# Latent attention: rotary's exchanged copy by a VectorE permutation of partitions instead of two output tiles of the query projection

## The reference, cut to what matters

```
cq  = rms_norm(h @ w_cq) (512 x 384);  ckv = rms_norm(h @ w_ckv) (512 x 256)
q   = cq @ even_w_uq      8 heads of 64 plain + 32 rotary features
k,v = ckv @ even_w_ukv    8 heads of 64 + 64; 32 rotary key features shared by all heads
rope(x): x1, x2 = halves of 16;  [x1*cos - x2*sin, x2*cos + x1*sin]
out = concat(plain heads, softmax(q k^T / sqrt(96), causal) v) @ even_w_out
```

## Time and profile before

| | before |
|---|---|
| median of 3 runs | 1935.88 us (1934.05 to 1936.56) |
| span of the profiled execution | 1933.6 us, 2.3 us under the median of the runs |
| the profiled execution's own time | not among the times shown; what lies around its span is about the 2.3 us |
| instructions | 30753 |
| TensorE matmuls busy | 1914.8 us (99%) |
| VectorE busy | 1156.5 us (60%) |
| ScalarE busy | 818.0 us (42%) |

### The profile page before, as it was taken

One profiled execution on the slowest core, in us unless ns is written; L12 is line 12 of the kernel. 1 busy time (PEld: TensorE's weight loads), 2 busy tenths in 40 slices (PEclk: granted clock), 3 DMA queues, 4 the chain that ended last, 5 costly groups with the idle time before them and its releaser, 6 DMA issues.

```text
span 1933.6 us, 30753 instructions
## 1 busy us (share of the span) xinstructions
PE 1914.8 (99%) x12210; PEld 1567.9 (81%) x12210; DVE 1156.5 (60%) x1891; ACT 818.0 (42%) x1327; POOL 27.4 (1%) x31
## 2 busy tenths in 40 slices
PE   9999999999999999999999999999999999999998
PEld 7777788888888877788888888877888778888887
DVE  6556577533655766657652555789988666425532
ACT  5457554333334454445332333465555543212232
POOL 0111000000000000000000000000000000000000
PEclk9999999999999999999999999999999999999999
DMA  6222123223223211131223222322111132322321
GB/s 222 77 77 77 49 83 107 78 98 109 89 88 128 71 45 66 66 109 66 87 87 109 104 83 82 112 67 79 56 62 46 66 109 87 109 87 88 108 87 66
DMA packets 30804, 168.61 MB, mean 87 GB/s; under 512 B 6456, under 2 KB 6616, under 8 KB 14816
## 3 DMA queue, kind: packets, MB, share of 16 engines
q1 hardware_dynamic: 25872, 161.69, 24.2%
q10 hardware_dynamic: 4816, 5.29, 0.9%
HBM read 163.78 MB, written 2.13 MB: 86 GB/s over the span
## 4 chain that ended last, share of the span: by engine, by line
PE 85%; DVE 8%; ACT 4%; issue 2%; DMA 1%; SPq 0%; DVEq 0%; ACTq 0%
PE bank L523 25%; PE bank L525 24%; PE bank L524 24%; PE bank L806 1%; ACT hH L1378 1%; PE bank L1172 1%; DVE hL L2194 1%; PE bank L989 1%; ACT wH L1378 1%; PE bank L818 1%; DVE x L2190 1%; PE bank L829 1%; PE bank L1013 1%; DVE wL L2117 1%; PE bank L1263 1%
## 5 line engine op out<-in xcount | busy, mean ns | idle before, releaser
L523 PE MATMUL bank<-hH,wH 128*128 128x512 f32 x1368 | 550.0, 402 | 1.8 <-DVE hL L2156 1.4
L525 PE MATMUL bank<-hH,wL 128*128 128x512 f32 x1368 | 532.1, 389 | 0.0
L524 PE MATMUL bank<-hL,wH 128*128 128x512 f32 x1368 | 531.4, 388 | 0.0
L1378 ACT ACTIVATE wH<-raw 128x2048 fp32r<-128x2048 f32 (+3 forms) x199 | 294.1, 1489 | 120.0 <-PE bank L525 104.8
L523 PEld LDWEIGHTS bank<-hH,wH 128*128 128x128 f32 x1368 | 257.2, 188 | 61.4 <-issue 9.1
L525 PEld LDWEIGHTS bank<-hH,wL 128*128 128x128 f32 x1368 | 256.8, 188 | 54.7
L2108 DVE TENSOR_TENSOR wL<-raw,wH 128x2048 fp32r<-128x2048 f32 x96 | 219.7, 2289 | 134.6 <-ACT wH L1378 134.6
L524 PEld LDWEIGHTS bank<-hL,wH 128*128 128x128 f32 x1368 | 257.5, 188 | 47.6 <-issue 1.2
L523 PE MATMUL bank<-mH,wH 128*128 128x512 f32 (+1 forms) x610 | 232.8, 382 | 0.0
L525 PE MATMUL bank<-mH,wL 128*128 128x512 f32 (+1 forms) x610 | 232.6, 381 | 0.0
L524 PE MATMUL bank<-mL,wH 128*128 128x512 f32 (+1 forms) x610 | 232.6, 381 | 0.0
(11 more groups left out here) (355 smaller groups left out, 2724.5 us busy)
## 6 DMA issues: line engine op xcount, KB each, us to landing
raw<-in_ffn_up SPq DMA_DIRECT2D x44, 1024.0 KB, 4.9
raw<-in_mlp_up SPq DMA_DIRECT2D x16, 1024.0 KB, 4.9
raw<-in_mlp_down SPq DMA_DIRECT2D x16, 1024.0 KB, 4.9
raw<-in_ffn_down SPq DMA_DIRECT2D x16, 768.0 KB, 4.3
raw<-in_odd_in SPq DMA_DIRECT2D x12, 1024.0 KB, 4.9
raw<-in_dn_qkv SPq DMA_DIRECT2D x12, 1024.0 KB, 5.0
raw<-in_ffn_down SPq DMA_DIRECT2D x16, 640.0 KB, 3.9
raw<-in_even_in SPq DMA_DIRECT2D x7, 1024.0 KB, 4.9
```

The source lines that it names most:

```text
L523: mm(out, a, c, start=first, stop=False, skip_group_check=joined)
L524: mm(out, a, d, start=False, stop=False, skip_group_check=joined)
L525: return mm(out, b, c, start=False, stop=last, skip_group_check=joined)
L1378: return nc.scalar.activation(out, in_, func, **kw)
```

## The change

The exchanged tiles go: the query projection has six output tiles, three for each unit, and a unit is 1152 columns wide. The exchanged copy is made by VectorE from the plain tile's bank, by `stream_shuffle` with the list 16..31, 0..15 within each quadrant of 32 partitions, and VectorE waits for it before the sine product, which then reads it from SBUF. The query projection's slots end at 178 instead of 184; everything behind is moved up: pairs 16, 17, 18 by two slots (172, 174, 176), pairs 19 and up and the output projection by three. Slots 178 to 180 have no projection step on TensorE. The second unit is needed at slot 169. Its split stays at slots 161 to 166. On VectorE rotary of group 0 moves to slot 163 (behind the division of pair 14) with its addition at once, that of group 1 to slot 175 with its addition at once, ahead of division 16 (176), the low part of group 3 (176) and minimum 18 (176). Bank 1 is now free for the next tile with the permutation's end (`rope.turned`).

```diff
-STREAMS = [("even_in", 9, 2048), ("even_ukv", 1, 2048), ("even_uq", 2, 1536), ("even_out", 4, 2048)]
+STREAMS = [("even_in", 9, 2048), ("even_ukv", 1, 2048), ("even_uq", 2, 1152), ("even_out", 4, 2048)]
-TILES = {"even_uq": 8, "even_ukv": 4 + 4}
+TILES = {"even_uq": 6, "even_ukv": 4 + 4}
...
-            return (48, 76, 104, 147)[g] + (7, 7, 7, 6)[g] * n if g < 4 else (174, 176, 178)[n] if m < 19 else 172 + 3 * (m - 16)
+            return (48, 76, 104, 147)[g] + (7, 7, 7, 6)[g] * n if g < 4 else (172, 174, 176)[n] if m < 19 else 169 + 3 * (m - 16)
...
-            return 16 * n - 14 if n < 9 else (130, 146, 161, 174, 186)[n - 9]
+            return 16 * n - 14 if n < 9 else (130, 146, 161, 171, 183)[n - 9]
...
-            for t in range(160, 184):
+            for t in range(160, 178):
                 j, k = (t - 160) // 3, (t - 160) % 3
-                n = UNIT0["even_uq"] + j // 4
+                n = UNIT0["even_uq"] + j // 3
                 pair_events(t)
                 if k == 0:
-                    if j % 4 == 0:
+                    if j % 3 == 0:
                         pe.wait_ge(w_split, n + 1)
-                    pe.wait_ge(*at(("ukv.out5", "ukv.out6", "ukv.out7", "rope.cos0", "rope.sin0", "uq.nope0", "uq.nope1", "rope.cos1")[j]))
-                c = slice(k * 512 + (j % 4) * P, k * 512 + (j % 4) * P + P)
+                    pe.wait_ge(*at(("ukv.out5", "ukv.out6", "ukv.out7", "rope.turned0", "uq.nope0", "uq.nope1")[j]))
+                c = slice(k * 384 + (j % 3) * P, k * 384 + (j % 3) * P + P)
...
-                if t < 220:
-                    n = (t - 184) // 3
-                    return None if t % 3 != 1 else (n // 8, n // 4 % 2, n % 4)
-                t -= 220
+                if t < 217:
+                    n = (t - 181) // 3
+                    return None if t < 181 or t % 3 != 1 else (n // 8, n // 4 % 2, n % 4)
+                t -= 217
...
-            for t in range(184, 240):
+            for t in range(178, 237):
...
-                if t in (170, 173, 182, 185):
-                    p = (170, 173, 182, 185).index(t)
-                    j = (2, 3, 6, 7)[p]
+                if t in (167, 170, 176, 179):
+                    p = (167, 170, 176, 179).index(t)
+                    j = (1, 2, 4, 5)[p]
...
-                turned, plain = (bank[uq_bank(4 * g + 1 - a_)][:] for a_ in range(2))
-                done("even_uq", 4 * g)
+                plain = bank[uq_bank(3 * g)][:]
+                done("even_uq", 3 * g)
                 if g:
                     dve.wait_ge(*at("rope.rotated0"))
                 stt(sq[:, g, :], plain, s, rope[:, 0, :], ALU.mult, ALU.mult).then_inc(*tick("rope_dve", f"rope.cos{g}"))
-                done("even_uq", 4 * g + 1)
-                stt(ss[:], turned, s, rope[:, 1, :], ALU.mult, ALU.mult).then_inc(*tick("rope_dve", f"rope.sin{g}"))
+                chain(nc.vector.stream_shuffle(ss[:], plain, [*range(16, 32), *range(16)]), "rope_dve", f"rope.turned{g}")
+                stt(ss[:], ss[:], s, rope[:, 1, :], ALU.mult, ALU.mult).then_inc(*tick("rope_dve", f"rope.sin{g}"))
...
-                if t in (166, 178):
-                    rotary((t - 166) // 12)
+                if t == 175:
+                    rotary(1)
                 for m in pairs_at(t, 4):
                     pair_divided(m)
+                if t == 163:
+                    rotary(0)
+                    rotated(0)
...
-                if t in (166, 178):
-                    rotated((t - 166) // 12)
+                if t == 175:
+                    rotated(1)
```

More of the change, by code:

```diff
@@ L943, in _ @@
                         pe.wait_ge(w_split, UNIT0["even_out"] + u + 1)
-                    pe.wait_ge(*at(("rope.sin1", "uq.nope2", "uq.nope3", "pair.biased31.1")[2 * u + tl]))
+                    pe.wait_ge(*at(("uq.nope3", "rope.turned1", "uq.nope2", "pair.biased31.1")[2 * u + tl]))
                 pe.wait_ge(*at(f"pair.out{k}"))
@@ L1656, in even_hi @@
             def even_hi(n, f):
-                act.wait_ge(mm_done, 2 * n - 2 if n <= 10 else TILE0["even_uq"] + 4 * (n - 11))
+                act.wait_ge(mm_done, 2 * n - 2 if n <= 10 else TILE0["even_uq"] + 3 * (n - 11))
                 hi_half(n, f)
@@ L1690, in rank_square @@
                 a(dst, cqRaw[:, k, :], ACT.Square).then_inc(*tick("norm_act", f"cq.sq{k}"))
-            for t in range(34, 240):
+            for t in range(34, 237):
                 for n in range(3, 14):
@@ L1696, in _ @@
                             even_hi(n, f)
-                if t == 222:
+                if t == 219:
                     act.wait_ge(*at("pair.scores31.1"))
@@ L1735, in _ @@
                     pair_hi(g)
-                if t == 188:
-                    act.wait_ge(*at("rope.sin1"))
+                if t == 185:
+                    act.wait_ge(*at("rope.turned1"))
                     a(small[:, 8:9], eps, ACT.Copy).then_inc(evac, TILES["even_ukv"] + TILES["even_uq"])
@@ L2479, in _ @@
                     for f in range(2):
-                        if (203 if (n, f) == (13, 1) else even_split_half(n, f) + 3 + f) == t:
+                        if (200 if (n, f) == (13, 1) else even_split_half(n, f) + 3 + f) == t:
                             lo_half(n, f)
-                if t == 226:
+                if t == 223:
                     lo_half(14, 0)
@@ L3068 @@
         four = heads[4 * g:4 * g + 4]
-        cols += [wq[:, 64:] for wq in four] + [np.concatenate([wq[:, 80:], wq[:, 64:80]], 1) for wq in four]
-        cols += [wq[:, :64] for wq in four]
-    arrays["even_uq"] = units(np.concatenate(cols, 1), 512)
+        cols += [wq[:, 64:] for wq in four] + [wq[:, :64] for wq in four]
+    arrays["even_uq"] = units(np.concatenate(cols, 1), 384)
     arrays["even_ukv"] = units(a["even_w_ukv"][0].reshape(256, H, 2, 64).transpose(0, 2, 1, 3).reshape(256, 1024), 1024)
```

## The result

The changed kernel takes 1941.68 us (median of 8 executions, 1939.86 to 1942.84), the kernel before, run beside it, 1936.62 us (median of 8, 1934.05 to 1938.49). The ratio is 1.0026, 95% interval 1.0017 to 1.0034: slower by 5.1 us, outside of the predicted range of 1932.6 to 1937.6. The profiled execution took 1942.52 us with a span of 1940.7, 7.1 us more than the span before. Around the span of every execution whose span is on record lie 1.7 to 1.9 us. So the profiled execution of the kernel before took about 1935.4 us, and what lies around its span is not the 2.3 us that the table of before has.

A forecast was written before the change was run, and what follows sets the result against it. TensorE, busy for 99% of the span, was taken as the bound: 4.1 us of steps and 0.3 of old idle time go, 4.1 of new idle time come, a 0.4 us lead, so 1935.5 us, range 1932.6 to 1937.6.

The forecast's parts named there:

- The sum over the stage's order: Latent-heads stage: 4.1 us of steps and 0.3 of old idle go, 4.1 of new idle come, lead 0.4 us.
- Permutation: VectorE, once per group: the 128x512 permutation takes 0.71 us, range 0.42 to 1.21, taken from the 32x32 transposition.
- rival (b): VectorE's permutation is dear and the kernel slower: 12 in 100 for above 0.91 us, 2 in 100 for above 2.9.
- Rotary: VectorE: cosine 0.60, permutation 0.71 + 0.04, sine 0.71, addition 0.60, together 2.66 us.
- The end of the weight unit: VectorE: the second half of the second weight unit's split ends at 162.81, where TensorE waits for it at slot 169.
- Stalls: New TensorE idle time: 2.5 us at slot 169, 0.5 before the scores of pair 19, 1.1 before pair 20.
- Rival (a): Stage: the saving comes through whole, 4.4 us go, 1931.5 us, 0.23% faster; 7 in 100, with half-way cases.
- rival (c): The stall at slot 169 lowers TensorE's clock; under 1 us at 1.2 GHz eats the 0.4; 3 in 100.
- 8 us at 1.2 GHz would be needed for 1939.5: TensorE's clock: every microsecond at 1.2 GHz loses half a microsecond of work, so 1939.5 us needs 8 us of it.
- the first stall: TensorE at slot 169 waits for the second half of VectorE's weight split, from 160.34 until 162.9: 2.5 us idle.
- a lead of 0.4: Followed along the path through the stage, the changed kernel is 0.4 us ahead: pair 21 at 182.4, not 182.83.
- I let the 0.4 us stand to the end: From slot 181 on: all engines' lists are unchanged, three slots sooner, so the 0.4 us lead stays: 1935.5 us.

The follow-up runs named there:

- e10: The changed kernel with 12 TensorE instructions (three one-column matmuls) put back at slot 190 and nothing else; 1939.15 us, ratio 1.0013.
- e3: The kernel before with the first half of the second unit's split done two times more on VectorE, so TensorE has to wait; 1940.58 us, ratio 1.0018.
- e4: The changed kernel with 36 TensorE instructions put back at 650 us, nine one-column sums in a norm of the second block; 1941.70 us, ratio 1.0026.
- e1: The changed kernel with GpSimd's clearing of qM and kM held until VectorE's division of pair 14 is done; 1938.86 us, ratio 1.0011.
- e6: The kernel before with 18 matmuls left out, 36 TensorE instructions fewer as in the changed kernel, every order kept; 1940.26 us, ratio 1.0018.
- e9: The changed kernel with GpSimd's clearing later, rotary of group 1 and one split half sooner, 12 TensorE instructions put back at slot 190; 1935.04 us, ratio 0.9993.
- e5: The changed kernel with GpSimd's clearing behind pair 14's division and 36 TensorE instructions (nine one-column matmuls) put back at slot 180; 1938.13 us, ratio 1.0006.
- e8: The changed kernel with GpSimd's clearing later, rotary of group 1 and one split half sooner, 36 TensorE instructions put back in the stage; 1935.71 us, ratio 0.9998.
- e2: The kernel before with only the last of three steps of each exchanged tile computed, 12 matmuls left out, all orders kept; 1936.76 us, ratio 1.0004.

## Why the prediction was wrong

**What held.** The sum over the stage's order was right in its steps. Permutation: 0.71 forecast, 0.73 measured, so rival (b) falls, whose point was 0.91. Rotary: 2.66, measured 2.71. The end of the weight unit: 162.8, measured 162.6. Stalls: 2.5, 0.5 and 1.1, measured 2.41, 0.30 and 0.84, each with the releaser named. The two later ones are shorter because TensorE itself was slower: from pair 17 to being ready for pair 19 it needed 7.61 us (169.79 to 177.40) where 7.3 was forecast, and from pair 19 to being ready for pair 20 1.70 where 1.46. Rival (a) falls with the 2.41 us: the saving did not come through. Up to pair 21 the sum's result is right too: the changed kernel's loss there, 1.3 us from its own start, is the 1.7 of clock less 0.4. To the end it isn't, even at full clock: e10's two executions without a fall are 0.9 us over those of before, of which its filling explains 0.7.

On the permutation's price the Trainium skill's figure (VectorE: DVE Perf Modes, The perf-mode tier table) gave an estimate of 0.60 us. The trace has 0.73 and decides. The same page (The DRAIN you can't avoid) gives no extra cost for a semaphore between two chained instructions. Here an instruction whose result is awaited is followed after 0.72 us (158.49 to 159.21), one whose result isn't after 0.61 (159.21 to 159.82), so the trace doesn't agree.

**First step that failed: rival (c), at 3 in 100.** The wait at slot 169 lowers the clock; it should have been part of the forecast. The text took the earlier trace rows, a wait of 2.12 us with full clock behind it, as evidence that such a wait is harmless. It was one execution, and the kernel before had a mean clock of 1.000 in only 15 of 83 others. The same wait is followed by the lower clock in the profiled executions of 9 of the 11 other kernels. The text also reckoned that 8 us at 1.2 GHz would be needed for 1939.5, without asking how long a fall lasts. Here each takes 1.7 us of work (3.4 us at half speed), in the stage as in the third block, but for the two long ones of e3 and e4. That makes the first stall 4.1 us and not 2.4, and all four traces with a wait of 2.3 to 2.5 us in the stage (the changed kernel, e3, e4, e10) have the fall. The 1.7 us turn a lead of 0.4 into a loss of 1.3, which is what pair 21 shows. By itself this step would have given 1937.2 us, within the range. e1 and e3 show it from both sides: without the wait the fall goes, with a wait in the kernel before it comes.

**Second step that failed: "I let the 0.4 us stand to the end".** The text reasoned that behind the stage all lists are the same, three slots sooner. The lead was gone at 187 us, in part by a wait of 0.23 us for ScalarE's copy y, which the kernel before doesn't have. And the instructions are the same, but there are 36 fewer ahead of them, and with that TensorE stands still in the third block. It costs 2.2 us of waiting and 1.7 us of clock, 3.9 us, which is more than half of the 7.1 us between the two spans, and no part of the forecast had a term for it. By the times it is 2.5 us (1941.68 to 1939.15, the changed kernel against e10), with e10's filling, 0.7 us, and its larger loss at 1228 (0.4 more) in the way. The 0.8 us at 1228 to 1232, a loss that only kernels with fewer instructions have, belong here too. e6 shows that taking instructions out is enough to bring the wait for issue up, e10 that 12 put back take it away.

**The sum as it came out**, in the span: 1.0 us at pair 21, that is 1.3 of the stage less the 0.3 by which this trace is ahead from its start; 0.4 more to 187 us; 0.8 at 1228 to 1232 us; 1.3 for that execution's clock fall behind the wait of 1296; 3.9 for the wait for issue and its clock fall; and 0.3 come back by 1400. Together 7.1, as between the spans. The profiled execution of before had no fall, and many of its others have some, so the medians show less, 5.1.

What stays open: what decides in one execution that the clock falls behind the same wait and in another that it doesn't; and how the chip places its fetches of instructions. That the fetch of a block causes the wait for issue is argued, not shown. The burst of small packets isn't what makes it. In e1 the block starts behind the burst, as the window 1339.3 to 1340 shows, where nothing else moves:

```profile
q8 instruction: 1, 0.02, 8.5%
```

It takes 0.95 us, as in the kernel before, and TensorE waits 2.08 us all the same. In e9 it takes 1.4 us, and TensorE doesn't wait. What goes with the wait in all twelve traces is when the block starts. In the four kernels with the wait it starts 0.0 to 0.8 us behind the start of the row of small matmuls, and TensorE goes on 1.3 to 1.4 us after the block has come. In the eight without the wait it starts 1.3 to 1.6 us behind the row's start. Why it needs 36 and not 24 instructions fewer was not looked into.

## What to carry to other kernels

A new wait of two microseconds on a TensorE that is otherwise never idle is to be priced at about 4 us and not at 2: the clock fell behind 17 of the 20 waits of 2.1 to 2.5 us in these twelve traces, and one trace in which it didn't is no evidence. Executions are best compared at the same mean clock, since the median of either kernel has falls in it. Taking instructions out of a long program isn't local: compare the starts of the same instruction in both traces to the very end, and where a jump stands far behind the change, look for a wait "issue" with an instruction transfer beside it; a handful of idle instructions may move it, at a price (12 took 0.7 us here, and the loss at another place grew by 0.4). Before putting work ahead of a due time on VectorE, look for what already slows that stretch: here a GpSimd clearing that could wait cost the division 2.4 us, and with it the stall.

## What the runs showed of the hardware that was not expected

- The clock fell behind 17 of 20 waits of 2.08 to 2.50 us, and behind 2.07 us of matmuls of one column, with a wait of 0.30 us shortly before (e5), though the profile counts the latter as busy; behind the same 2.07 us in e8 it stayed full. It didn't fall behind waits of 0.42 us (e1, e9) or 1.14 us (e2). A matmul of 512 columns then comes every 0.43 us, not every 0.23. Of the 19 falls in the twelve traces (those at the very end of the span left out) 17 cost 1.7 us of work and two 3.4 us (e3, e4).
- It doesn't fall in every execution: mean clock 1.000 in 2 of 10 (e3), 1 of 10 (e5), 2 of 11 (e10), and in 15 of 83 of the kernel before. The Trainium skill (TensorE: Matmul & The Clock Gate, What's actually happening) says of a kernel's start that the number of matmuls at the lower clock differs from run to run; in these runs it differs in the middle of a kernel too.
- TensorE stood still for 2.1 to 2.4 us, with no semaphore to show for it, in all four kernels with 36 TensorE instructions fewer, and in none of the other eight. A block of 16 KB of instructions landed 1.3 to 1.4 us before it went on. Such a block took from 0.95 us (e1) to 1.4 us (the changed kernel, e6, e9) at this place, and its length doesn't go with the wait.
